# Sixteen conditioning products on another engine, and block-wise order around three norms, in a two-layer encoder trunk

## Chip, cores and metric

One core of a Trainium2 chip (the program uses 1 core). Time is device microseconds from first to last instruction as the runs give it, the median of several runs; lower is better. All numbers are fp32 (matmul operands are split into a high and a low part of type fp32r).

## What is computed

A trunk of two layers over 256 tokens of width 1024. Both layers are modulated by a conditioning vector:

```python
cond = jax.nn.silu(c)
mod = cond @ ada_w[l] + ada_b[l]                       # (1024) @ (1024, 6*1024)
sh_a, sc_a, g_a, sh_f, sc_f, g_f = jnp.split(mod, 6, axis=-1)
h = modulate(rms_norm(x, norm_attn[l]), sh_a, sc_a)    # h*(1+scale) + shift
y = diff_attention(h, ...)   if l == 0 else window_attention(h, ..., k_band, v_band)
x = x + g_a * y
h = modulate(rms_norm(x, norm_ffn[l]), sh_f, sc_f)
y = swiglu(h, ffn_w_in, ffn_w_out) if l == 0 else moe_swiglu(h, ...)   # 8 experts, top 2
x = x + g_f * y
# after layer 0: shared keys and values from modulate(rms_norm(x, kv_norm), ...) @ kv_w
```

The products of the title are `cond @ ada_w` for two of these rows: `sh_f` of layer 0 and `g_f` of layer 1. Each is a sum over eight pieces of 128x1024: piece k is scaled by a column of `condT` and added into a 128x1024 row block, which TensorE then sums over partitions with a matrix of ones (`mod_sums`).

## The kernel before

Five engines run programs of their own, ordered by semaphores alone; within an engine the written order holds. Tokens lie in two blocks of 128 (i = 0, 1).

**Weights.** SP loads everything of size into a ring of 12 slots of 128x1024 (`WRAW`), in the order that `ring_order()` writes out; a slot is reloaded when its reader is done (`slot_read`). ScalarE copies a unit to fp32r (`hi`, L675, into 6 slots of `WHI`), VectorE subtracts (`lo`, L1052, `WLO`), and TensorE runs three matmuls per product (`split_mm`, all at L1667: high x high, high x low, low x high). Units are numbered through: 0 to 23 query/key/value, 24 to 31 W_O of layer 0 (`U_WO`), 32 on the feed-forward (`U_FF`), then `U_KV`, `U_BQ` (queries of layer 1), `U_BO`, `U_MOE`. `hi` of a unit waits until TensorE has used the unit six before it.

**Conditioning pieces** share the ring: the places `(c, k)` are piece k of chunk c, `("gate_f", k)` those of layer 1's gate. VectorE multiplies and adds in one operation (L1066 `early_product`, L1076 `gate_products`, L1087 for the pieces that GpSimd loads into its own four slots); some pieces TensorE takes itself (`scale_pieces` in the first attention; in heads 9 to 12 it gives their slots free).

**Norms.** For each block: `residual` (L1214, L1215), the sum of squares and root on ScalarE (`norm_root`), `scaled` (L1114), `norm` (L1124), transposes on TensorE (`ht_transposes`, L1717), high parts on ScalarE (`ht_his`, L734) and low parts on VectorE (`ht_los`, L1135, or L1137 with a scale). `project_by_block` runs block 0's matmuls ahead of block 1's, so that block 0's residual and norm can begin early.

**Attention.** Heads n = 0 to 15 (8 heads, two row blocks) in a pipeline: TensorE logits for n + 3, VectorE bias and maximum for n + 2 (`biased`, L1168, L1172), ScalarE exponentials for n + 2 (L754), VectorE totals of n (L1182; in layer 0 also L1186 and L1188, which combine the two softmax maps), TensorE transposes (L1790), ScalarE copies (`copy_pt`, L764), TensorE products with V. `keep_clock` issues matmuls whose result nobody reads.

**Feed-forward.** 11 steps of 256 columns: in-projection (4 units), SiLU on ScalarE (L879), product on VectorE (L1348), transposes (L1936), high part (L883) and low part (L1352), out-projection (2 units). VectorE works off 64 further conditioning products in these steps; when one chunk is complete (`FF_SUMS`), TensorE sums it in two halves (`mod_half`) that ScalarE copies back (L889).

GpSimd issues some loads and clears rows with memsets (L569 to L622); it computes nothing else before the experts.

## Time and profile before

| | us |
|---|---|
| median of 3 runs | 1558.24 (1553.27 to 1561.35) |
| profiled execution | 1554.59, span of its instructions 1552.8 |
| TensorE busy | 1480.1 (95%), mean granted clock 0.979 of 2.4 GHz |
| VectorE, ScalarE, GpSimd busy | 1301.7 (84%), 980.2 (63%), 89.0 (6%) |
| DMA | 318 GB/s over the span |

Busy times are shares of the whole span and don't say which engine a stage waits for. That is read from the chain of work that ended last, from the table of stretches and from the waits within one stretch. A busy TensorE may still run at its lower clock: the mean granted clock of the stretch tells.

### The profile page before, as it was taken

How to read it: one execution, taken by the hardware profiler on the slowest of the kernel's cores; microseconds unless marked ns; L12 is line 12 of the kernel's file. 1: busy time of each engine (PE TensorE's matmuls, PEld its weight loads, DVE VectorE, ACT ScalarE, POOL GpSimd, SP SyncE). 2: the span in 40 equal slices, each digit the busy share in tenths (PEclk: the TensorE clock that was granted, in tenths of full speed). 3: DMA queues.
4: the chain of work that ended last, by engine and by line, in shares of the span. 5: the costliest groups of instructions: out<-in, count | busy, mean ns of one | idle time of the engine just before them, and what ended most of it. 6: DMA issues, size and time to landing. Idle time of an engine off the chain costs nothing.

```text
span 1552.8 us, 22121 instructions
## 1 busy us (share of the span) xinstructions
PE 1480.1 (95%) x6514; PEld 1159.6 (75%) x6514; DVE 1301.7 (84%) x1390; ACT 980.2 (63%) x1248; POOL 89.0 (6%) x127
## 2 busy tenths in 40 slices
PE   5997899999889889999999999999999999999998
PEld 2774677777567668888888888888888888888886
DVE  6787878887865687998888888889889888889897
ACT  2468343443544346777777776777677767777774
POOL 3000121120100001000000000000000000000100
PEclk9999999999995989999999999999999999999999
DMA  9983699998740279999999999999999999999993
GB/s 352 334 337 101 194 338 365 352 360 294 172 140 14 82 270 327 365 363 395 361 358 390 371 356 388 370 365 372 374 372 367 377 364 369 368 366 363 397 393 137
DMA packets 212225, 494.33 MB, mean 318 GB/s; under 512 B 16433, under 2 KB 39185, under 8 KB 212177
## 3 DMA queue, kind: packets, MB, share of 16 engines
q1 hardware_dynamic: 196848, 440.46, 78.3%
q0 software_dynamic: 14528, 51.22, 9.4%
q10 hardware_dynamic: 802, 2.06, 0.4%
q8 instruction: 25, 0.41, 0.1%
q14 instruction: 22, 0.18, 0.0%
HBM read 487.13 MB, written 6.55 MB: 318 GB/s over the span
## 4 chain that ended last, share of the span: by engine, by line
PE 84%; DVE 8%; DMA 3%; ACT 2%; issue 1%; SPq 0%; ACTq 0%; DVEq 0%
PE PS L1667 80%; DVE WLO L1052 2%; DMA WRAW<-in_a_w_qkv 2%; PE PS L2151 2%; DMA WRAW<-in_ada_w 1%; DVE MOD L1066 1%; PE PS L1790 1%; ACT WHI L675 1%; DVE HT_LO L1135 1%; DVE MOD L1076 1%; PE PS L1717 0%; PE PS L2129 0%; DVE ss L1142 0%; SPq L432 0%; DVE X L1215 0%
## 5 line engine op out<-in xcount | busy, mean ns | idle before, releaser
L1052 DVE TENSOR_TENSOR WLO<-WRAW,WHI 128x1024 fp32r<-128x1024 f32 x790 | 916.1, 1218 | 60.0 <-ACT WHI L675 59.7
L675 ACT ACTIVATE WHI<-WRAW 128x1024 fp32r<-128x1024 f32 x790 | 779.0, 1052 | 92.7 <-PE PS L1667 65.6
L1667 PE MATMUL PS<-WHI,HT_HI 128*128 128x512 f32 x1280 | 518.4, 405 | 25.7 <-DVE WLO L1052 17.8
L1667 PE MATMUL PS<-WLO,HT_HI 128*128 128x512 f32 x1280 | 509.2, 398 | 0.0
L1667 PE MATMUL PS<-WHI,HT_LO 128*128 128x512 f32 x1280 | 435.9, 397 | 0.0
L1667 PEld LDWEIGHTS PS<-WHI,HT_HI 128*128 128x128 f32 x1280 | 242.0, 189 | 88.0 <-DVE WLO L1052 21.2
L1667 PEld LDWEIGHTS PS<-WHI,HT_LO 128*128 128x128 f32 x1280 | 241.9, 189 | 59.0
L1667 PEld LDWEIGHTS PS<-WLO,HT_HI 128*128 128x128 f32 x1280 | 242.6, 190 | 54.7 <-issue 0.5
L1667 PE MATMUL PS<-WHI,AT_HI 128*128 128x512 f32 x536 | 216.7, 404 | 2.8 <-DVE AT_LO L1582 1.4
L1667 PE MATMUL PS<-WLO,AT_HI 128*128 128x512 f32 x536 | 211.7, 395 | 0.0
L1667 PE MATMUL PS<-WHI,AT_LO 128*128 128x512 f32 x536 | 211.7, 395 | 0.0
L994 ACT ACTIVATE AT_HI<-PS 128x512 fp32r<-128x512 f32 x56 | 33.5, 599 | 197.4 <-PE PS L2151 197.4
L1667 PEld LDWEIGHTS PS<-WHI,AT_HI 128*128 128x128 f32 x536 | 100.6, 188 | 30.0 <-issue 2.9
L1667 PEld LDWEIGHTS PS<-WLO,AT_HI 128*128 128x128 f32 x536 | 100.6, 188 | 26.8 <-issue 2.9
L1667 PEld LDWEIGHTS PS<-WHI,AT_LO 128*128 128x128 f32 x536 | 100.5, 188 | 24.5
L1582 DVE TENSOR_TENSOR AT_LO<-PS,AT_HI 128x512 fp32r<-128x512 f32 x56 | 38.8, 692 | 92.8 <-ACT AT_HI L994 92.8
L1087 DVE SCALAR_TENSOR_TENSOR MOD<-SHR,condT,MOD 128x1024 f32<-128x1024 f32 x64 | 81.9, 1279 | 2.1 <-DVE MOD L1087 0.5
L643 POOL DMA_DIRECT2D y_rows<-MOD x7 | 4.0, 574 | 792.8 <-DVE MOD L1561 792.8
L1667 PE MATMUL PS<-MOD,CST 128*128 128x512 f32 x64 | 34.9, 657 | 12.1 <-DVE MOD L1066 6.8
L1066 DVE SCALAR_TENSOR_TENSOR MOD<-WRAW,condT,MOD 128x1024 f32<-128x1024 f32 x32 | 41.0, 1281 | 6.5 <-DMA WRAW<-in_ada_w 5.7
L883 ACT ACTIVATE AT_HI<-PS 128x512 fp32r<-128x512 f32 x11 | 6.6, 599 | 60.4 <-PE PS L1936 60.4
L990 ACT ACTIVATE MOD<-PS 128x512 f32<-128x512 f32 x56 | 33.5, 599 | 15.3 <-PE PS L1667 15.3
(215 smaller groups left out, 841.8 us busy)
## 6 DMA issues: line engine op xcount, KB each, us to landing
WRAW<-in_moe_w_in SPq DMA_DIRECT2D x448, 512.0 KB, 6.4
WRAW<-in_moe_w_out SPq DMA_DIRECT2D x224, 512.0 KB, 5.5
WRAW<-in_ada_w SPq DMA_DIRECT2D x48, 512.0 KB, 8.8
SHR<-in_ada_w POOLq DMA_DIRECT2D x48, 512.0 KB, 6.6
WRAW<-in_ffn_w_in SPq DMA_DIRECT2D x88, 256.0 KB, 5.9
WRAW<-in_a_w_qkv SPq DMA_DIRECT2D x24, 512.0 KB, 15.4
WRAW<-in_ffn_w_out SPq DMA_DIRECT2D x22, 512.0 KB, 6.9
SHR<-in_kv_ada_w POOLq DMA_DIRECT2D x16, 512.0 KB, 6.3
```

Of the source, the lines that this page charges most:

```text
L675: nc.scalar.activation(WHI[:, u.split(k), :], WRAW[:, u.raw(k), :], ACT.Copy).then_inc(w_hi, 1)
L990: nc.scalar.activation(ESIL, PS[:, 0, :], ACT.Silu).then_inc(e_silu, 1)
L994: nc.scalar.activation(AT_HI[:, :], PS[:, 2, :], ACT.Copy).then_inc(e_at_hi, 1)
L1052: V_.tensor_tensor(WLO[:, u.split(k), :], WRAW[:, u.raw(k), :], f32(WHI[:, u.split(k), :]), ALU.subtract).then_inc(w_lo, 1)
L1066: V_.scalar_tensor_tensor(row, piece, condT[:, k:k + 1], row, ALU.mult, ALU.add).then_inc(ada_used, 1)
L1076: V_.scalar_tensor_tensor(row, WRAW[:, place % RAW_SLOTS, :], condT[:, k:k + 1], row, ALU.mult, ALU.add).then_inc(ada_used, 1)
L1087: V_.scalar_tensor_tensor(row, ADA[:, k % ADA_SLOTS, :], condT[:, k:k + 1], row, ALU.mult, ALU.add).then_inc(ada_used, 1)
L1135: V_.tensor_tensor(dst, src, high, ALU.subtract).then_inc(ht_lo, 1)
L1582: V_.tensor_tensor(AT_LO[:, :], PS[:, 2, :], f32(AT_HI[:, :]), ALU.subtract).then_inc(e_at, 1)
L1667: return nc.tensor.matmul(out, a, b, start=start, stop=stop)
L1790: last = nc.tensor.transpose(PS[:, 4 + n % 2, at:at + P], s_buf(a, n)[:, m, kt * P:(kt + 1) * P], ident)
L2151: last = nc.tensor.transpose(PS[:, 2, c * P:(c + 1) * P], EACT[:, c * P:(c + 1) * P], ident)
```

## The change

1. The eight pieces of layer 0's feed-forward shift, `(3, k)`, move ahead of W_O's units 28 to 31 in the ring, and their products from VectorE to GpSimd, into the first attention: a multiplication in place, then an addition to the row, with a wait on GpSimd's own semaphore after each. The eight `gate_f` products also move to GpSimd, into the second attention.
2. TensorE sums the shift row after block (0, 5) of W_O (`shift_sum`), no longer after (1, 2).
3. The first feed-forward step's SiLU and product run by block, and step 1's first two units are multiplied for each block as it is ready (`f_in_first`).
4. ScalarE copies the second half of each summed chunk (`mod_half(c, 1)`) behind the first two high parts of the next step.
5. Around the three norms of layer 0's end, the keys and layer 1's queries, the low parts of weights and of block 0 are reordered, on ScalarE and VectorE.
6. In the second attention Q's block 1 is transposed in two halves through one bank; in both, the square-root table is loaded one head earlier.

The core of the diff:

```diff
-    order += list(range(U_WO + 4, U_FF)) + [(3, k) for k in range(KT)]
+    order += [(3, k) for k in range(KT)] + list(range(U_WO + 4, U_FF))
     order += list(range(U_FF, U_BO + 5)) + [("gate_f", k) for k in range(KT)]
...
+POOL_PIECES = [(3, k) for k in range(KT)] + [("gate_f", k) for k in range(KT)]
+DVE_PIECES = [what for what in RING if isinstance(what, tuple) and what not in PE_PIECES and what not in POOL_PIECES]
...
-                elif isinstance(what, tuple):
-                    sp.wait_ge(ada_used, DVE_FF + what[1] + 1)
+                elif what in POOL_PIECES:
+                    sp.wait_ge(pool_used, POOL_PIECES.index(what) + 1)
                 elif place >= 0:
                     sp.wait_ge(w_lo, (what if what is not None else U_MOE + place - len(RING)) + 1)
...
+                    for piece in range(KT):
+                        load_piece((3, piece), t["ada_w"][0], 3 * D)
                 load(u, k, t["a_w_o"][0, k * P:(k + 1) * P, :])
-            for k in range(KT):
-                load_piece((3, k), t["ada_w"][0], 3 * D)
...
+            def pool_products(first, row):
+                for k in range(KT):
+                    n = first + k
+                    place = PLACE[POOL_PIECES[n]]
+                    pool.wait_ge(w_landed[place % RAW_SLOTS], landed_at(place))
+                    piece = WRAW[:, place % RAW_SLOTS, :]
+                    nc.gpsimd.tensor_scalar(piece, piece, condT[:, k:k + 1], None, ALU.mult).then_inc(pool_scaled, 1)
+                    pool.wait_ge(pool_scaled, n + 1)
+                    nc.gpsimd.tensor_tensor(row, row, piece, ALU.add).then_inc(pool_used, 1)
+                    pool.wait_ge(pool_used, n + 1)
+            pool.wait_ge(modb_landed, 32)
+            pool_products(0, MOD[:, MOD0[3], :])
             pool.wait_ge(attn["A"]["pt_psum"], TB * HEADS)
...
+            pool.wait_ge(attn["B"]["biased"], 1)
+            pool_products(KT, MOD[:, MOD1[5], :])
             pool.wait_ge(attn["B"]["pt_psum"], TB * HEADS)
...
-                    if n == 1 and a == "B":
-                        transposed(10, lambda n: Q[:, 1, n * 512:n * 512 + 512], 3, (6, 7), qkt_psum)
+                    if n in (1, 2) and a == "B":
+                        transposed(9 + n, lambda _: Q[:, 1, (n - 1) * 512:n * 512], 3, (7,), qkt_psum)
...
+                    if n == 13:
                         load_table(ACT.Sqrt)
...
             hi(u, 30, 31)
+            mod_rows(MOD0[3], 2, 4)
             hi_ff_in(u, (32,), 0, True)
             norm_root(0, 1)
-            mod_rows(MOD0[3], 2, 4)
             hi_ff_in(u, (33, 34), 0, True)
             ht_his(2, BLOCKS[:2])
             hi_ff_in(u, (35,), 0, True)
             norm_root(1, 2)
+            load_table(ACT.Silu)
             ht_his(2, BLOCKS[2:])
-            load_table(ACT.Silu)
...
+                u, it, k0 = Units(first + step // 2 * RAW_SLOTS), step // 2, 6 * (step % 2)
+                if step:
+                    hi_ff_in(u, range(k0, k0 + 2), it)
+                if step - 1 in FF_SUMS:
+                    mod_half(FF_SUMS[step - 1], 1)
+                hi_ff_in(u, range(k0 + 2, k0 + 4), it)
+                f_at(step + 1)
+                hi(u, k0 + 4, k0 + 5)
+                f_silu(u, k0 + 3)
+                if step in FF_SUMS:
+                    mod_half(FF_SUMS[step], 0)
             first = U_FF + FF_IN
-            for it in range((FF_STEPS - 1) // 2):
-                f_pair(it)
+            hi_ff_in(Units(first), range(0, 2), 0)
+            for i, (sem_in, n, sem_out) in enumerate(((f_block, 1, silu_block), (w_used, U_FF + FF_IN, silu_ready))):
+                act.wait_ge(sem_in, n)
+                nc.scalar.activation(FSIL[:, i, :], PS[:, i, 0:FC], ACT.Silu).then_inc(sem_out, 1)
+            for step in range(FF_STEPS - 1):
+                f_step(step)
             u = Units(U_KV - FF_OUT)
             hi(u, 0, 1)
+            mod_half(FF_SUMS[FF_STEPS - 2], 1)
+            hi(u, 2, 3)
             f_at(FF_STEPS)
-            hi(u, *range(2, 6))
+            hi(u, 4, 5)
...
-            ht_his(4, BLOCKS[:2])
             act.wait_ge(kv_block, 1)
             nc.scalar.activation(KV[:, 0, :], PS[:, 4, :], ACT.Copy).then_inc(kv_copied, 1)
-            ht_his(4, BLOCKS[2:])
+            ht_his(4, BLOCKS[:2])
+            hi(u, 2)
             act.wait_ge(w_used, U_BQ)
             nc.scalar.activation(KV[:, 1, :], PS[:, 6, :], ACT.Copy).then_inc(kv_copied, 1)
-            hi(u, 2, 3)
+            ht_his(4, BLOCKS[2:])
+            hi(u, 3, 4)
             for i in range(TB):
                 act.wait_ge(kv_copied, i + 1)
                 block_squares(i, KV[:, i, 0:256], 7)
-            hi(u, 4, 5, 6)
+            hi(u, 5, 6, 7)
             transposed(0, lambda n: KBT[:, 2 * n:2 * n + 2, :].rearrange("p j k -> p (j k)"), 4,
                        range(0, 2), kbt_psum)
-            hi(u, 7)
...
-            lo_and_products(29, 1)
             o_scale(1)
-            for piece in islice(rest, 1):
-                early_product(piece)
+            lo(u, 29)
             ht_los(1, BLOCKS[2:], gcol[:, 2:3])
-            for piece in islice(rest, 2):
-                early_product(piece)
-            lo_and_products(30, 1)
-            lo_and_products(31, 3)
+            lo(u, 30, 31)
...
-            lo(u, 32)
+            lo(u, 32, 33)
             ht_los(2, BLOCKS[:2])
-            lo(u, 33)
+            lo(u, 34)
             dve.wait_ge(w_used, U_FF)
             residual(1, MOD0[2])
+            lo(u, 35)
             scaled(1, H, MOD0[4], 2, 2)
-            lo(u, 34)
             rms(1)
             norm(1, H, MOD[:, MOD0[3], :])
-            lo(u, 35)
+            lo(u, 36)
             ht_los(2, BLOCKS[2:])
+            lo(u, 37)
...
+            for i, (ready, done) in enumerate(((silu_block, act_block), (silu_ready, act_ready))):
+                dve.wait_ge(ready, 1)
+                V_.tensor_tensor(FACT[:, i, :], FSIL[:, i, :], PS[:, i, FC:2 * FC], ALU.mult).then_inc(done, 1)
...
+                    if step or k >= 2:
+                        lo(u, k0 + k)
...
             lo(u, 0, 1)
-            f_at(FF_STEPS)
             dve.wait_ge(mod_ready, MOD_READY_EARLY + 2 * LATE_SHIFT_F)
             fold(MODKV[1], MOD[:, MODKV[1], :], 3)
-            lo(u, 2)
+            lo(u, 2, 3)
+            f_at(FF_STEPS)
+            lo(u, 4, 5)
             dve.wait_ge(block_out, 2)
             residual(0, MOD0[5])
             scaled(0, H, MODKV[1], 3, 3)
             rms(0)
             norm(0, H, MOD[:, MODKV[0], :])
-            lo(u, 3)
-            ht_los(3, BLOCKS[:2])
             dve.wait_ge(w_used, U_KV)
             residual(1, MOD0[5])
+            ht_los(3, BLOCKS[:2])
             scaled(1, H, MODKV[1], 3, 4)
-            lo(u, 4)
             rms(1)
             norm(1, H, MOD[:, MODKV[0], :])
-            lo(u, 5)
+            fold(MOD1[1], MOD[:, MOD1[1], :], 4)
             ht_los(3, BLOCKS[2:])
-            fold(MOD1[1], MOD[:, MOD1[1], :], 4)
             u = Units(U_BQ)
-            for i in range(TB):
-                scaled(i, Q, MOD1[1], 4, 3 + i)
-                norm(i, Q, MOD[:, MOD1[0], :])
-                lo(u, i)
-            ht_los(4)
-            lo(u, 2, 3)
+            scaled(0, Q, MOD1[1], 4, 3)
+            norm(0, Q, MOD[:, MOD1[0], :])
+            lo(u, 0)
+            ht_los(4, BLOCKS[:2])
+            lo(u, 1)
+            scaled(1, Q, MOD1[1], 4, 4)
+            norm(1, Q, MOD[:, MOD1[0], :])
+            lo(u, 2)
+            ht_los(4, BLOCKS[2:])
+            lo(u, 3, 4)
...
-            lo(u, *range(4, 8))
+            lo(u, 5, 6, 7)
...
-            lo(u, 13)
-            gate_products(0, 1)
-            lo(u, 14)
-            gate_products(2, 3)
-            lo(u, 15)
+            lo(u, 13, 14, 15)
...
-            gate_products(4, 5)
-            lo(u, 18)
-            gate_products(6, 7)
-            lo(u, 19)
+            lo(u, 18, 19)
...
-                    if n == 1 and a == "B":
+                    if n in (1, 2) and a == "B":
                         pe.wait_ge(qk_norm, 6)
-                        block_transposes(Q, 1, 6, qkt_psum)
+                        if n == 2:
+                            pe.wait_ge(qkt_ready, 11)
+                        for h in range(4):
+                            c = (n - 1) * 512 + h * P
+                            last = nc.tensor.transpose(PS[:, 7, h * P:(h + 1) * P], Q[:, 1, c:c + P], ident)
+                        last.then_inc(qkt_psum, 1)
+                    if n == 3 and a == "B":
                         pe.wait_ge(qkt_ready, 12)
                     if n:
                         products(n - 1)
                     if a == "A":
                         scale_pieces(n)
-                    elif 2 <= n < HEADS:
+                    elif 3 <= n < HEADS:
                         keep_clock(7, 1)
...
+            def shift_sum():
+                pe.wait_ge(ht_lo, 8)
+                mod_sums(KT, MOD0[3], 2, pool_used)
             project_by_block(Units(U_WO), 4, 4, {
                 (0, 2): second_rows,
-                (1, 2): lambda: mod_sums(DVE_EARLY, MOD0[3], 2),
+                (0, 5): shift_sum,
                 (1, 6): lambda: ht_transposes(H, h_parts(2, BLOCKS[:2]))})
...
+            def f_in_first(u):
+                for i, ready in enumerate((act_block, act_ready)):
+                    pe.wait_ge(ready, 1)
+                    for k in range(2):
+                        split_ready(u, k)
+                        s, rows = u.split(k), slice(i * P, i * P + P)
+                        for kt in range(2):
+                            cols, kk = slice(kt * 512, kt * 512 + 512), 2 * k + kt
+                            last = split_mm(PS[:, i, :], HT_HI[:, kk, rows], HT_LO[:, kk, rows], WHI[:, s, cols],
+                                            WLO[:, s, cols], kk == 0, False)
+                        if i:
+                            last.then_inc(w_used, 1)
...
+                    if it or b:
+                        pe.wait_ge(act_ready, it * 2 + (b + 1))
+                        f_in(u, 6 * b, (0, 1))
+                    else:
+                        f_in_first(u)
...
+                if k == 1:
                     ht_transposes(Q, h_parts(4, BLOCKS[:2]))
             ht_transposes(Q, h_parts(4, BLOCKS[2:]))
...
+            mod_sums(len(POOL_PIECES), LATE_SLOTS[LATE_GATE_F], 2, pool_used)
```

## Rows read from the trace of the kernel before

**Rows 1.** The page, chain that ended last: shares of the span by engine.

```profile
PE 84%; DVE 8%; DMA 3%; ACT 2%; issue 1%; SPq 0%; ACTq 0%; DVEq 0%
```

**Rows 2.** Stretches: length, busy of PE, PEld, DVE, ACT, POOL (instructions); clock; DMA.

```profile
107.00:155.00 48.00, 38.69 (x200) 22.45 (x198) 37.59 (x91) 36.55 (x112) 0.57 (x1) 1.00 0.45 161
155.00:212.00 57.00, 48.47 (x201) 37.05 (x201) 45.84 (x48) 21.37 (x30) 12.35 (x14) 0.94 0.69 223
212.00:391.00 179.00, 178.08 (x761) 138.62 (x760) 151.66 (x139) 74.11 (x90) 30.09 (x57) 1.00 0.94 342
391.00:458.00 67.00, 54.28 (x235) 40.24 (x234) 48.59 (x60) 33.46 (x48) 6.84 (x8) 0.95 0.64 170
458.00:511.00 53.00, 48.52 (x238) 36.67 (x236) 27.31 (x69) 29.53 (x91) 0.57 (x1) 0.68 0.11 33
511.00:566.00 55.00, 46.54 (x212) 35.44 (x212) 44.40 (x72) 20.59 (x31) 1.09 (x2) 0.88 0.43 144
566.00:1552.80 986.80, 977.86 (x4338) 787.59 (x4338) 863.81 (x829) 717.34 (x787) 21.49 (x18) 1.00 0.98 360
```

**Rows 3.** Waits of PE in 155 to 212: total us, times, longest.

```profile
PE PS L1667 <- DVE WLO L1052: 6.8, 3, 3.2
PE PS L1667 <- DVE MOD L1066: 0.9, 1, 0.9
```

**Rows 4.** Waits of PE in 212 to 391.

```profile
PE PS L1667 <- DVE WLO L1052: 0.9, 5, 0.2
```

**Rows 5.** Waits of PE in 391 to 458.

```profile
PE PS L1667 <- DVE WLO L1052: 8.0, 3, 3.1
PE PS L1667 <- ACT MOD L931: 1.2, 1, 1.2
```

**Rows 6.** Waits of PE in 458 to 511, then in 511 to 566.

```profile
PE PS L1667 <- ACT Q L742: 1.9, 1, 1.9
PE PS L1667 <- DVE WLO L1052: 2.0, 1, 2.0
```

**Rows 7.** DVE by line, 155 to 185: busy us, mean ns, idle.

```profile
L1066 DVE SCALAR_TENSOR_TENSOR MOD<-WRAW,condT,MOD 128x1024 f32<-128x1024 f32 x8 | 10.2, 1280 | 0.3
```

**Rows 8.** Timeline of DVE and PE: start us, us, engine, line, operation.

```profile
175.36 1.22 DVE L1214 TENSOR_TENSOR H<-PS,MOD 128x1024 f32<-128x1024 f32 x1
...
553.31 0.29 PE L2088 MATMUL PS<-CST,W 8*128 8x8 f32 x2
...
555.16 0.17 DVE L1461 TENSOR_TENSOR rt<-PS,rb 128x16 f32<-128x16 f32 x1
```

**Rows 9.** Groups of DVE by line, 511 to 566.

```profile
L1052 DVE TENSOR_TENSOR WLO<-WRAW,WHI 128x1024 fp32r<-128x1024 f32 x9 | 10.9, 1217 | 0.1
L1076 DVE SCALAR_TENSOR_TENSOR MOD<-WRAW,condT,MOD 128x1024 f32<-128x1024 f32 x8 | 10.2, 1281 | 0.4
L1124 DVE SCALAR_TENSOR_TENSOR H<-H,nx,MOD 128x512 f32<-128x512 f32 x4 | 2.8, 749 | 0.1
```

**Rows 10.** SP and ACT in first attention; landing times of loads, 130 to 152.

```profile
137.22 2.68 SPq L432 DMA_DIRECT2D WRAW<-in_ada_w  x2
WRAW<-in_ada_w SPq DMA_DIRECT2D x4, 512.0 KB, 3.7
139.07 1.05 ACT L675 ACTIVATE WHI<-WRAW 128x1024 fp32r<-128x1024 f32 x1
148.20 1.28 ACT L696 ACT_TABLE_LOAD   x1
```

**Rows 11.** Timeline of POOL: its memsets.

```profile
160.73 4.46 POOL L600 MEMSET MOD<- 128x2048 f32 x3 [11.68 <-DVE Q L1151]
191.91 2.67 POOL L602 MEMSET MOD<- 128x3072 f32 x1 [26.71 <-DVE H L1124]
```

**Rows 12.** Groups of DVE by line in first attention, 107 to 155.

```profile
L1168 DVE TENSOR_TENSOR S<-PS,SHR 128x256 f32<-128x256 f32 (+1 forms) x8 | 4.4, 556 | 2.6 <-PE PS L1667 2.3
L1188 DVE SCALAR_TENSOR_TENSOR S<-S,sm 128x128 f32<-128x128 f32 (+1 forms) x8 | 3.3, 418 | 0.3
```

69 lines of the change are left out of this document (24 added, 45 removed).

## The prediction

> **What bounds the kernel now.** I read the chain that ended last first: TensorE carries 84% of it, VectorE 8% [rows 1]. So a microsecond counts only where TensorE stands still or runs at its lower clock. The table of stretches shows where that is [rows 2]: the experts (566 to 1552.8) are full (977.9 of 986.8 us busy, clock 1.00), and the change doesn't touch them. The feed-forward steps are full too (178.1 of 179.0). What is loose lies in five stretches: first attention (107 to 155, 9.3 us of TensorE idle), its output projection and the first feed-forward block (155 to 212: 8.5 idle, mean clock 0.94), key/value and query projection (391 to 458: 12.7 idle, clock 0.95), second attention (458 to 511: 4.5 idle, clock 0.68) and its output projection with the router (511 to 566: 8.5 idle, clock 0.88). A mean clock of 0.94 over 57 us is 3.4 us of full-speed time lost, 0.95 over 67 us also 3.4; the two levels are 2.4 and 1.2 GHz. The pitch of matmuls at full clock comes from the full stretch: 178.08 us over 761, 0.234 us each [rows 2]. Then I asked TensorE's waits in each stretch who ended them [rows 3 to 6]: nearly all are low parts (`lo`, L1052) that VectorE makes late.
>
> **Feed-forward's shift products to GpSimd, and the output projection (155 to 212).** Removed from VectorE: eight products, 10.2 us, mean 1280 ns [rows 7]. That isn't 10.2 us of path: TensorE stood 0.9 us for the last of them and 6.8 for low parts [rows 3], the shortest of them behind a product, the two long ones (up to 3.2) from the order around the norm and the first SiLU. `residual(0)` began at 175.36 [rows 8], after the products and the fold, though its matmuls were done some 2 us earlier. With the products gone and low parts 32 and 33 done ahead, and with the first SiLU split so that step 1's first matmuls (`f_in_first`) fill the time of SiLU and product, the waits of 6.8 and 0.9 and the 3.4 us of lost clock are up for gain: 11.1. What is late next: `f_in_block(0, 2)` is followed by the transposes of block 1's norm. From the end of W_O, VectorE needs two residual operations, a low part, a scaling and a norm: 4 x 1.22 + 2 x 0.75 = 6.4 us [rows 9]; TensorE has three blocks of 6 matmuls, 18 x 0.234 = 4.2. So a wait of 2.2 remains, and up to 3.8 with `lo(34)` and `ht_los` ahead of the residual; I take 3.0, and as such a wait was followed by the low clock before, half of the lost clock, 1.7. **Term: 11.1 - 4.7 = -6.4** (bounds -11 and -3).
>
> **What moves in the queues for it.** On SP the eight shift pieces pass ahead of W_O units 28 to 31. These then hold ring places that are free only when TensorE has used the four scale pieces in heads 9 to 12; before, four of the shift pieces waited there, the first issued at 137.22 and landing 3.7 us later [rows 10]. So unit 28 lands at 140.9, while ScalarE took it at 139.07 [rows 10]: ScalarE's strict order puts 1.9 us of waiting in front of the next heads' exponentials and PT copies. It runs two heads ahead, so the bounds are 0 and +1.9; I take +1.5. The feed-forward loads behind them on SP no longer wait for VectorE's low parts and products, but stand behind GpSimd's. Loading the square-root table one head earlier takes 1.28 us [rows 10] from between the last head's transposes and products: -1.2 (bounds -1.3 and 0). On GpSimd's queue the products pass ahead of the wait for the gain `norm_ffn`; they cost nothing as long as they end before attention does.
>
> **How long GpSimd takes, and what that does to VectorE.** No row shows GpSimd reading. The nearest are its memsets: 2.67 us for 3072 columns, 0.89 for 1024 [rows 11]. A product is now a multiplication (one in, one out) and an addition (two in, one out): with all streams overlapped 2 x 0.89 = 1.8 us, with each stream paid singly 5 x 0.89 = 4.5. I take the middle, 3.1, so 25 us for eight (14 to 36). The Trainium skill (GPSIMD Engine Reference, § 3.1) gives 4497 ns for an addition of 2048 columns, by estimate 2.25 us here, and § 4.1 there advises VectorE for such work; the sum would be the same by it, and no run here shows it yet. First set: the pieces land about when attention begins, 107, and their sum stands behind eight blocks of 6 matmuls of W_O, 155 + 8 x 1.4 = 166: 59 us, 7.4 per product. Second: 458 to 553, 12 per product. Both hide.
>
> But attention's VectorE work runs beside it. VectorE's products kept 1280 ns beside GpSimd's memsets (4.46 us at 160.73) and 1281 in a stretch where GpSimd did next to nothing [rows 7, 9, 11]: writing alone disturbs nothing, and a pure reading of the rows gives 0. Reading isn't shown. In first attention each head has an L1186 and an L1188 (0.42 us), which read two operands from SBUF [rows 12]. If these wait once per head for half of a mean GpSimd operation (0.8 us) over the ten heads that 25 us cover, that is 8 us, less about half of the idle time VectorE has there (2.6 us in the eight heads of one buffer [rows 12], so some 4 in ten): +4. Bounds 0 and +14 (below). **Term of first attention: 1.5 - 1.2 + 4 = +4.3.**
>
> **Sums of the feed-forward steps.** `mod_half(c, 1)` on ScalarE goes behind the first two `hi` of the next step. TensorE's waits for low parts in these steps are 0.9 us in all [rows 4]. **-0.9** (0 to -2).
>
> **Key/value and query projection.** The three long waits for low parts (8.0 us) and one for the copy of KV (1.2) [rows 5] go: `lo(4)` comes before the head norms, `hi(7)` before the copies of the transposed keys, and ScalarE copies KV ahead of block 1's high parts. With shorter gaps the 3.4 us of clock return. New waits: `ht_los(3)` of block 0 now stands behind both operations of `residual(1)`, 2.4 us, and ahead of it one low part less, 1.2: +1.2. Between the norms of Q's two blocks VectorE has two low parts, two `ht_los`, a scaling and a norm of two halves: 3 x 1.22 + 4 x 0.75 = 6.7 us (each half operation at the norm's 0.75 [rows 9]), while TensorE has 12 matmuls, 2.8, and 8 shorter transposes, some 4 us: +2.7. One of the low-clock stretches I leave: +1.2. **Term: -12.6 + 5.1 = -7.5** (-12.6 to -4).
>
> **Second attention.** The half-by-half transposes of Q's block 1 remove the 1.9 us wait for the copies [rows 6]. Heads run on TensorE at a clock of 0.68 on average [rows 2], so nothing else there ends a wait, and GpSimd's products meet no VectorE operation with two SBUF inputs but `lo(12)`. **-1.9** (-4 to 0).
>
> **Gate products to GpSimd (511 to 566).** Again 10.2 us leave VectorE [rows 9], and of the path: the 2.0 us for `lo(15)` behind four of them [rows 6], and the start of the router's logits, which came at 555.16 behind the last four, while the transposes that feed them were issued at 553.31 and took 0.29 [rows 8]: 1.4. The wait for the norm of block 1 stays. **-3.4** (-3.4 to -2). The expert weights that wait for these ring places land earlier; no wait there was for a load, so 0.
>
> **Sum:** 4.3 - 6.4 - 0.9 - 7.5 - 1.9 - 3.4 = **-15.8 us**. On the profiled execution of 1554.59 (span 1552.8) that is 1538.8; on the median of the runs, 1558.24 (3.65 above it, among runs from 1553.27 to 1561.35), 1542.4. I forecast **1540**, between the two.
>
> **Rivals.** *A: GpSimd's reading and VectorE's two-operand operations shut each other out for whole instructions.* Then each head's L1186 waits for the rest of one GpSimd operation (0.8 us) and L1188 for a whole one (1.55), as the two stand close enough for GpSimd to step in between: 2.35 a head, over some seven heads until the 25 us are worked off, 16, less 2 of idle: +14 instead of +4, **1550**. For it: the operations are there in every head; against it: rows 7 and 9, which only show writing. The Trainium skill (SBUF — State Buffer, § Who interferes with whom) states this exclusion for a VectorE instruction with two SBUF inputs against a GpSimd instruction that reads SBUF, and none against one that only writes; with the second half the trace agrees (1280 against 1281 ns). *B, the slower side: a GpSimd product takes over 10 us.* Then the first set ends after 166 and TensorE waits in the middle of W_O: 8 x (T - 7.4). At T = 10.7 this is 26 us, which turns the sum into +10: some **1566**; from T = 9.4 on the change is a loss. That would be 12 memset passes per product, against it the 0.89 of rows 11. *C: the change doesn't do what it says in the two norm stretches*: TensorE stops at the next norm instead of at low parts, and the clock falls there as before. Half of 6.4 and 7.5 is then lost, +7: **1547**. For it: the mean clocks of 0.94 and 0.95 stand beside waits of 3 us, and one of my new waits is that long. *D: no exclusion (-4) and no lost clock or wait left behind the new norms (-5):* **1531**.
>
> **Chances.** Forecast 0.49, A 0.20, B 0.06, C 0.18, D 0.07. The range 1527 to 1552 leaves out B, the worse third of A and a little below D: about 0.16. What can be told from no change is about 0.5%, 7.8 us: under 1550.4 is faster. Of A a bit under half is faster, of C most: faster 0.49 + 0.07 + 0.09 + 0.15 = 0.80, same 0.14, slower 0.06.
>
> **What would show it.** GpSimd rows of 128x1024 beside first attention, each pair near 3.1 us, ending before 155; L1186 or L1188 with idle time ahead of them ended by nothing on the chain (A). `hi` of unit 28 some 2 us late behind its load. In the W_O stretch no wait for L1066, one of about 3 us for L1124 (C if longer, with the clock down). In 391 to 458 no wait over 1 us for L1052. Router logits right behind their transposes. Wrong would be: experts at another pace, a longer second attention, or the sum of the shift rows as the releaser of a TensorE wait (B).

## The result, and the profile after

The changed kernel takes 1543.86 us in the median (1529.26 to 1553.59), the kernel before 1559.71 in the same series. Ratio **0.9888, 95% interval 0.9866 to 0.991**: faster by some 17 us. The ratio leaves out the two slowest runs of the changed kernel (1553.55 and 1553.59), which count as slow; with them the medians differ by 15.9 us. The forecast was 1540 with 1527 to 1552. What I had not foreseen is the spread: 24 us for the changed kernel, where the kernel before has 12 (1553.27 to 1565.04, one outlier apart). The first profiled execution of the changed kernel (1553.59) was its slowest, so the rows below, wherever they are called "after", are from another execution of the same kernel, `e1_again`, with a span of 1538.5.

The stretches of the kernel after, cut where the same stages now begin; columns as in [rows 2]:

```profile
107.00:160.00 53.00, 39.33 (x196) 22.33 (x194) 45.06 (x89) 35.07 (x111) 44.53 (x17) 0.97 0.47 170
160.00:217.00 57.00, 51.66 (x224) 40.73 (x225) 40.14 (x46) 24.52 (x35) 12.88 (x15) 0.97 0.65 215
217.00:395.00 178.00, 176.42 (x757) 138.21 (x756) 157.78 (x144) 77.49 (x94) 32.85 (x61) 1.00 0.97 350
395.00:447.00 52.00, 47.18 (x215) 35.77 (x213) 40.08 (x53) 27.54 (x41) 3.74 (x4) 0.97 0.62 167
447.00:499.00 52.00, 49.23 (x236) 38.11 (x235) 27.27 (x68) 29.52 (x91) 42.21 (x17) 0.64 0.35 121
499.00:554.00 55.00, 47.94 (x227) 37.09 (x228) 36.45 (x66) 22.50 (x33) 1.08 (x2) 0.91 0.33 106
```

Against [rows 2], first attention is longer (53 us to the first matmul of the output projection, 48 before), GpSimd is busy for 44.5 us of it, and the projection of keys, values and queries is much shorter. Second attention has the lowest clock, 0.64. TensorE's waits after, in four groups: output projection with the first feed-forward block (160 to 217), feed-forward, key/value and query projection, and the stage behind second attention (499.3 to 576.8):

```profile
PE PS L1726 <- DVE H L1140: 2.7, 1, 2.7
PE PS L1676 <- DVE HT_LO L1151: 2.2, 1, 2.2
PE PS L1676 <- DVE HT_LO L1153: 1.2, 1, 1.2
...
PE PS L1676 <- DVE AT_LO L1364: 1.6, 1, 1.6
...
PE PS L1676 <- DVE HT_LO L1151: 2.4, 1, 2.4
PE PS L1726 <- DVE Q L1140: 1.8, 1, 1.8
PE PS L1726 <- DVE H L1140: 0.6, 1, 0.6
...
PE PS L1726 <- DVE H L1140: 3.2, 1, 3.2
PE PS L1676 <- DVE HT_LO L1151: 2.2, 2, 1.2
PE PS L1676 <- DVE HT_LO L1576: 2.2, 1, 2.2
...
```

Not one wait for weights' low parts (L1052 before, L1078 now) is left of the 6.8, 0.9, 8.0 and 2.0 us of [rows 3 to 6], nor one for the shift products. What stands there now are waits for norms (L1140) and for the low parts of transposes.

Where the time went is clearest in the length of each stage, from the first matmul of one to the first matmul of the next in TensorE's timeline. The borders are: first matmul of the output projection; first and last matmul of the feed-forward's output blocks; clock matmuls ahead of second attention; first matmul of its output projection; first expert output. "Rest" runs to the end of the span. The kernels are described below.

| profiled execution | to output proj. | + first FF block | FF | KV, Q | attention B | to experts | rest | span |
|---|---|---|---|---|---|---|---|---|
| before | 155.1 | 62.6 | 180.2 | 61.0 | 52.7 | 81.1 | 960.2 | 1552.8 |
| after, first | 168.6 | 55.9 | 178.9 | 54.4 | 55.7 | 77.0 | 961.4 | 1551.8 |
| after (e1_again) | 160.4 | 56.7 | 178.5 | 51.8 | 51.9 | 77.6 | 961.6 | 1538.5 |
| e2_shift_dve | 154.5 | 59.8 | 178.7 | 51.6 | 54.0 | 77.5 | 961.4 | 1537.5 |
| e3_gate_dve | 165.0 | 55.9 | 178.8 | 51.6 | 54.0 | 81.2 | 961.3 | 1547.7 |
| e7_kv_undone | 161.5 | 56.7 | 178.2 | 61.1 | **37.0** | 77.2 | 960.0 | 1531.6 |
| e8_fill | 165.2 | 55.9 | 179.1 | 54.4 | **37.0** | 76.0 | 961.5 | 1529.0 |
| e9_best | 156.2 | 60.6 | 178.5 | 51.8 | **37.0** | 76.3 | 961.5 | 1521.9 |
| e10_before_fill | 158.5 | 62.7 | 180.2 | 61.1 | 52.7 | 81.1 | 961.6 | 1557.8 |

### The profile page after: what moved, and what is told of

Read it like the earlier page. It is cut to its first block, busy times and chain, and to the rows that moved or that the text cites. A ratio compares the mean times of both kernels' runs of the same rounds, so it can differ in the third digit from the quotient of the medians.

```text
span 1551.8 us, 22142 instructions
## 1 busy us (share of the span) xinstructions
PE 1488.7 (96%) x6513; PEld 1170.5 (75%) x6513; DVE 1291.8 (83%) x1375; ACT 980.5 (63%) x1249; POOL 175.0 (11%) x159
## 4 chain that ended last, share of the span: by engine, by line
PE 89%; DVE 6%; DMA 2%; ACT 1%; issue 1%; SPq 0%; POOL 0%; DVEq 0%; ACTq 0%
PE PS L1676 85%; PE PS L2190 2%; DMA WRAW<-in_ada_w 1%; PE PS L1799 1%; DVE WLO L1078 1%; PE PS L1726 1%; DMA SHR<-in_kv_ada_w 1%; DVE MOD L1092 1%; DVE MOD L1103 0%; DVE sm L1202 0%; DVE HT_LO L1151 0%; PE PS L2168 0%; DVE X L1231 0%; DVE ss L1158 0%; DVE H L1230 0%
## 5 line engine op out<-in xcount | busy, mean ns | idle before, releaser
L1078 DVE TENSOR_TENSOR WLO<-WRAW,WHI 128x1024 fp32r<-128x1024 f32 x790 | 915.6, 1217 | 43.4 <-ACT WHI L696 42.9
L606 POOL TENSOR_SCALAR WRAW<-WRAW,condT 128x1024 f32<-128x1024 f32 x16 | 47.5, 2967 | 74.3 <-DMA WRAW<-in_ada_w 37.2
```

Of the source, the lines that this page charges most:

```text
L606: nc.gpsimd.tensor_scalar(piece, piece, condT[:, k:k + 1], None, ALU.mult).then_inc(pool_scaled, 1)
L1078: V_.tensor_tensor(WLO[:, u.split(k), :], WRAW[:, u.raw(k), :], f32(WHI[:, u.split(k), :]), ALU.subtract).then_inc(w_lo, 1)
```

## The experiments

Three questions were open: what lengthens first attention, whether each stage's gain belongs to the part that I gave it to, and where the spread comes from. The theories that the text names by a letter are set out in the expectations.

**1. The same kernel again, and one part undone at a time.**

> The changed kernel once more, for another profiled execution. In the profile at hand first attention ends 13.5 us later than before (output projection begins at 168.6 instead of 155.1), at a mean granted clock of 0.89. Theory R (GpSimd's reading holds up VectorE's operations with two SBUF operands, the heads come slower and the clock falls at chance places): the time again between 1529 and 1553 us, ratio 0.985 to 0.993, and a faster execution has the same VectorE gaps in first attention but a higher clock there. Rival Q (what is lost is the late load of output-projection unit 28 and the order on SP): the gap in front of hi(28) on ScalarE is the largest one there, 2 us or more, whatever the clock.

Ratio 0.9918 (0.9889 to 0.9948), median of ten runs 1546.30 us (1536.14 to 1551.59). The wait for unit 28 is there, 1.11 us ahead of `hi(28)` on ScalarE, but it isn't the largest gap. TensorE's waits in first attention, after (107 to 160) and, in the last two lines, before (107 to 155):

```profile
PE PS L1799 <- DVE MOD L1204: 6.4, 5, 2.2
PE PS L1799 <- DVE S L1204: 3.8, 3, 1.6
PE PS L1799 <- ACT H L801: 1.6, 1, 1.6
...
PE PS L1790 <- DVE MOD L1188: 3.0, 3, 1.1
PE PS L1790 <- DVE S L1188: 1.8, 2, 1.2
...
```

10.2 us in eight places for VectorE's combination of a head, where the kernel before waits 4.8 in five for the same step (L1188). This execution has such gaps as the first profiled one has (10.7 us in seven places there), and a mean clock of 0.97, where the first has 0.83 over its longer attention (107 to 168; the 0.89 of the expectation is the mean up to 155). That speaks for theory R.

`e2_shift_dve` gives the shift products back to VectorE (the core of the edit; the order on SP and the place of the row's sum go back too):

```diff
-POOL_PIECES = [(3, k) for k in range(KT)] + [("gate_f", k) for k in range(KT)]
+POOL_PIECES = [("gate_f", k) for k in range(KT)]
...
+            lo_and_products(29, 1)
             o_scale(1)
-            lo(u, 29)
...
-            lo(u, 30, 31)
...
+            lo_and_products(30, 1)
+            lo_and_products(31, 3)
```

> The changed kernel with the eight shift products (3, k) back on VectorE behind attention, with their pieces behind output-projection units 28 to 31 on SP and their row sum in block 1's pass, as before the change; gate products stay on GpSimd, everything else stays changed. Theory R: first attention is as before (output projection begins at about 154 to 156 us), and the stage after it loses the 6.7 us that it gained; together about 7 us faster than the changed kernel: ratio to the kernel before about 0.984. If the attention's loss of some 10 us is not due to the GpSimd products at all (the earlier square-root table, say): output projection begins at 165 or later and the time is 6 us above the changed kernel's, ratio 0.993.

Ratio 0.9842 (0.9766 to 0.9918), 1535.71 us. First attention is as before (154.5 against 155.1), the next stage takes 59.8 instead of 56.7. So of the 5.9 us that this stage gained, the products' leaving is worth 3.1; the other 2.8 come from the order and the halved first SiLU, which this kernel keeps (a remainder; they were not undone singly). Against that, first attention loses 6.0 by these two executions, one low-clock stretch of some 3 us (124 to 127) in `e1_again` included. **On balance the shift products on GpSimd cost 2.9 us**, more where the clock falls. I had expected 7. The ratio is the expected one, 0.984, but four runs between 1522.35 and 1543.68 don't settle it; the stages do.

`e3_gate_dve` gives the gate products back:

```diff
-            lo(u, 13, 14, 15)
+            lo(u, 13)
+            gate_products(0, 1)
+            lo(u, 14)
+            gate_products(2, 3)
+            lo(u, 15)
```

> The changed kernel with the eight gate products back on VectorE in the output projection behind second attention, as before the change; shift products stay on GpSimd. My forecast's term for these was -3.4 us (2.0 for lo(15), 1.4 for the router's logits) and nothing lost in second attention: so 3.4 us slower than the changed kernel, ratio to the kernel before about 0.991. Rival: GpSimd's reading costs second attention about 3 us as well (it ended at 512.3 against 510.4 with a wait of 1.9 gone): then equal to the changed kernel within 1 us, and second attention ends at about 509.

The stage behind second attention takes 81.2 us again, 81.1 before and 77.6 with the products on GpSimd: the 3.6 us belong to them. TensorE's wait of 2.0 for the low part is back. Second attention takes 54.0 without GpSimd's work and 51.9 and 55.7 with it, and VectorE's scaling of a head's output there (L1210, one operand in PSUM) takes 292 ns with GpSimd's products beside it and 291 without: nothing shows that GpSimd costs time there. The total doesn't tell it: ratio 0.9918 (0.9888 to 0.9947), equal to the changed kernel's, which is what the rival said. But the interval is 9 us wide, the effect 3.6, for a reason that comes in part 3. TensorE's waits behind second attention in this run:

```profile
PE PS L1693 <- DVE WLO L1078: 2.0, 1, 2.0
...
PE PS L1693 <- DVE rt L1499: 1.1, 1, 1.1
```

**2. What lengthens first attention.** `e4_write_only` puts six writes in place of a multiplication and an addition in the first eight products; the shift row is left out (in the three diffs of this part the semaphores, and in the first two the condition that keeps the gate products as they are, are left out):

```diff
-                    nc.gpsimd.tensor_scalar(piece, piece, condT[:, k:k + 1], None, ALU.mult).then_inc(pool_scaled, 1)
-                    nc.gpsimd.tensor_tensor(row, row, piece, ALU.add).then_inc(pool_used, 1)
+                    for m in range(6):
+                            pool.memset(piece, 0.0)
```

> In the changed kernel each of the first eight GpSimd products (a multiplication and an addition, 5.4 us) is replaced by six writes of a constant into the same piece, some 0.89 us each, 5.4 us; the products of the shift row of block 0's feed-forward are left out. SP's order, the ring places and when they come free stay the same. Theory R (reading is what hurts): first attention is back to its length before, output projection begins at 154 to 157 us, some 10 to 13 us faster than the changed kernel, ratio to the kernel before 0.979 to 0.983. Rival Q (late load of unit 28, order on SP), or a GpSimd that disturbs by writing too: it still begins at 165 or later, and the ratio is that of the changed kernel, 0.989.

VectorE's groups between 117 and 160 us, first of the kernel after (L1202 is the scalar step of each head's totals, one column of two operands; L1204 the combination), then of this one, then GpSimd's own groups after and here (105 to 170):

```profile
L1202 DVE SCALAR_TENSOR_TENSOR sm<-sm,neglam 128x1 f32<-128x1 f32 x15 | 10.7, 711 | 0.5
L1204 DVE SCALAR_TENSOR_TENSOR S<-S,sm 128x256 f32<-128x256 f32 (+1 forms) x7 | 3.1, 437 | 0.2
...
L1209 DVE SCALAR_TENSOR_TENSOR sm<-sm,neglam 128x1 f32<-128x1 f32 x15 | 3.3, 219 | 0.5
...
L606 POOL TENSOR_SCALAR WRAW<-WRAW,condT 128x1024 f32<-128x1024 f32 x8 | 25.1, 3138 | 37.4 <-DMA WRAW<-in_ada_w 36.7
L608 POOL TENSOR_TENSOR MOD<-MOD,WRAW 128x1024 f32<-128x1024 f32 x8 | 18.8, 2350 | 0.7
...
L610 POOL MEMSET WRAW<- 128x1024 f32 x48 | 45.7, 952 | 40.1 <-DMA WRAW<-in_ada_w 37.4
```

GpSimd is as busy (45.7 us against 43.9), and the one-column step falls from 711 ns back to 219. The last transposes of first attention end at 148.6, as in `e2_shift_dve` (148.3), 154.3 with the products. So it is the reading, and the late load of unit 28, which is in this kernel too (1.31 us of waiting on ScalarE), costs some 0.3 us, an estimate from these two ends. The output projection began at 158.6, not at 154 to 157: the granted clock was 0.50 from 150 to 156. Ratio 0.9885 (0.983 to 0.9941), 1537.56 us, not the 0.979 to 0.983 expected. The verdict rests on the rows, not on the time. It holds over all fourteen profiles of this document: the last transposes end at 148.2 to 150.4 in the six in which GpSimd reads nothing beside first attention, and at 154.3 to 159.9 in the eight in which it does.

Which instruction of GpSimd does it? VectorE at one head, then GpSimd beside it, after:

```profile
120.67 0.42 DVE L1188 TENSOR_REDUCE sm<-S 128x2 f32<-128x256 f32 x1
121.01 0.15 DVE L1198 RECIPROCAL sm<-sm 128x2 f32<-128x2 f32 x1
121.20 1.57 DVE L1202 SCALAR_TENSOR_TENSOR sm<-sm,neglam 128x1 f32<-128x1 f32 x1
122.80 0.37 DVE L1204 SCALAR_TENSOR_TENSOR MOD<-MOD,sm 128x128 f32<-128x128 f32 x1
...
117.37 2.95 POOL L606 TENSOR_SCALAR WRAW<-WRAW,condT 128x1024 f32<-128x1024 f32 x1
120.40 2.35 POOL L608 TENSOR_TENSOR MOD<-MOD,WRAW 128x1024 f32<-128x1024 f32 x1
122.85 2.95 POOL L606 TENSOR_SCALAR WRAW<-WRAW,condT 128x1024 f32<-128x1024 f32 x1
```

One-operand instructions (L1188, L1198) run on beside the addition, with the lengths that they have before (0.42 and 0.15 us). L1202 ends at 122.77, when the addition ends at 122.75. The blocked time is inside the instruction's own duration, not idle time ahead of it, which was the sign that I had named for rival A. All seven L1202 that met an addition took 1.07 to 1.57 us, all nine that met a multiplication 0.22. So I expected that two inputs on both sides are needed, and tested it with multiplications alone (`e5_one_input`; the shift row is left out):

```diff
-                    nc.gpsimd.tensor_tensor(row, row, piece, ALU.add).then_inc(pool_used, 1)
+                    nc.gpsimd.tensor_scalar(piece, piece, condT[:, k:k + 1], None, ALU.mult).then_inc(pool_used, 1)
```

> In the changed kernel, GpSimd's addition (two inputs from SBUF) of the first eight products is replaced by a second multiplication of the piece in place (one input from SBUF); the shift row of block 0's feed-forward is so left out. GpSimd is busy as long or longer: 2 x 2.85 against 2.85 + 2.35 us a product. Theory R1, from the trace of the changed kernel (L1202 took 0.22 us in each of the nine heads in which it met GpSimd's multiplication, and 1.07 to 1.57 in the seven in which it met the addition, until the addition's end): only instructions with two inputs on both engines shut each other out. Then L1202 keeps 0.22 us in all heads, the last transposes of first attention end at about 148.5 us as with writes alone (148.57) instead of 154 to 160, and the ratio to the kernel before is about 0.983. Rival R2 (any GpSimd instruction that reads): L1202 is 0.7 us on average or more, the last transposes end at 154 or later, ratio 0.99.

R1 fell in this form. The step takes 452 ns in the mean, between both theories, and the combinations (L1210 here) are longer too:

```profile
L1208 DVE SCALAR_TENSOR_TENSOR sm<-sm,neglam 128x1 f32<-128x1 f32 x15 | 6.8, 452 | 0.5
L1210 DVE SCALAR_TENSOR_TENSOR S<-S,sm 128x256 f32<-128x256 f32 (+1 forms) x7 | 4.4, 633 | 0.2
...
133.50 2.86 POOL L609 TENSOR_SCALAR WRAW<-WRAW,condT 128x1024 f32<-128x1024 f32 x1
133.75 1.15 DVE L1210 SCALAR_TENSOR_TENSOR S<-S,sm 128x256 f32<-128x256 f32 x1
...
136.45 2.85 POOL L607 TENSOR_SCALAR WRAW<-WRAW,condT 128x1024 f32<-128x1024 f32 x1
136.58 1.25 DVE L1210 SCALAR_TENSOR_TENSOR S<-S,sm 128x256 f32<-128x256 f32 x1
```

Take the instruction's own 0.48 off its end: 133.75 + 1.15 - 0.48 = 134.42, or 0.92 after the multiplication's start; 136.58 + 1.25 - 0.48 = 137.35, 0.90 after it. So it is in all nine cases of this run (0.90 to 0.95); those that came over 0.9 us after a multiplication's start were not held up. The multiplication shuts VectorE out for its first 0.9 of 2.85 us, the addition for 2.15 of 2.35 (the same working on the 13 cases of the two profiles of the changed kernel: 2.14 to 2.16). These shares go by GpSimd's spans in the profile, which its legend calls rough; from start to start the two take 3.03 and 2.45 in the rows above. In the profile of the changed kernel that I had read, VectorE's two-operand steps came 0.05 us ahead of a multiplication or 1.2 us and more after its start, never in between; so it looked harmless. (In the first profile two combinations came within 0.1 us of a multiplication's start; they took 1.16 and 1.23 instead of 0.35, which gives 0.90 and 0.91.) Ratio 0.9872 (0.9817 to 0.9928). The last transposes end at 154.6, not at R1's 148.5, with the clock at half from 135 to 139 and again from 152.

If the lock lasts as long as an instruction, shorter additions should help. `e6_add_parts`:

```diff
+                    for c in range(4):
+                        cols = slice(c * D // 4, (c + 1) * D // 4)
-                        nc.gpsimd.tensor_tensor(row, row, piece, ALU.add)
+                        nc.gpsimd.tensor_tensor(row[:, cols], row[:, cols], piece[:, cols], ALU.add)
```

> In the changed kernel each of GpSimd's sixteen additions is cut into four of 256 columns, one behind the other; what is computed stays. If a VectorE instruction with two SBUF inputs only waits for the GpSimd instruction that is running, L1202 waits 0.6 us at most (a quarter of 2.35) instead of up to 2.35, its mean falls from 0.71 to about 0.4, first attention's last transposes end at about 150 instead of 154, and the kernel is about 4 us faster than the changed kernel: ratio to the kernel before 0.984 to 0.987. Rival: the next part begins before VectorE comes in, so L1202 still waits for the last part, at a cost per part of its own (some 0.1 us each): ends at 154 or later, ratio 0.99 or above.

The step's mean fell to 409 ns as expected, but the combinations behind it took 686 and 911 instead of 424 and 437: VectorE gets in between two parts and is shut out again by the next. All three groups together cost 18.0 us against 17.2 with whole additions (9.6 undisturbed), and an addition takes 4 x 0.76 = 3.0 us. The last transposes end at 159.3, with the clock down three times before that (from 120, 127 and 140). Ratio 0.9876 (0.9818 to 0.9933), 1540.91 us: no gain that can be told.

**3. The key/value projection, and the spread.** `e7_kv_undone` puts back the order before on three engines, for example on VectorE:

```diff
-            scaled(0, Q, MOD1[1], 4, 3)
-            norm(0, Q, MOD[:, MOD1[0], :])
-            lo(u, 0)
-            ht_los(4, BLOCKS[:2])
-            lo(u, 1)
+            for i in range(TB):
+                scaled(i, Q, MOD1[1], 4, 3 + i)
+                norm(i, Q, MOD[:, MOD1[0], :])
+                lo(u, i)
+            ht_los(4)
```

> The changed kernel with VectorE's, ScalarE's and TensorE's order in the key/value and query projection as before the change (from the last feed-forward step's high parts to the copies of the transposed keys); all else stays changed. My term for this stage was -7.5 us; by the two profiles it is some 9 (from the last feed-forward output matmul to the clock matmuls of second attention: 61.0 us before, 51.8 after). If that is the order's own worth: the stage takes 60 to 62 us again and the kernel is 9 us slower than the changed kernel, ratio to the kernel before 0.995 to 0.998. If most of it were the granted clock's chance: 56 us or less, ratio 0.992 or below.

The stage takes 61.1 us again, with the waits of [rows 5] (8.1 for low parts, 1.2 for the copy). So the 9.2 us are the order's own. (It is 6.6 in the executions in which this stage took 54.4 us, with a second low-clock stretch in it: the first profile and `e8_fill`.) The ratio, 0.9933 (0.9902 to 0.9964), is 2 us worse than that of `e1_again` and 7 worse than that of the first series, in an interval of 10: the total doesn't settle it. And the profiled execution is the shortest so far, 1531.6: in it second attention took 37.0 us instead of 52 to 56. The two stretches of second attention, after and here (length, TensorE busy, clock, DMA share, GB/s):

```profile
447.43:499.31 51.88, 48.80 (x233) 0.64 0.35 119
...
457.47:494.43 36.96, 32.76 (x234) 1.00 0.35 115
```

The same heads, with GpSimd's products beside them in both (41.8 and 35.8 us busy); the granted clock is 0.64 in one and 1.00 in the other. At 0.50 TensorE is busy almost without a break (25.00 of 25.00 us in a row further down) and bounds the heads. Where the clock falls, it does so soon after the first head's start; after:

```profile
453.02 0.44 PE L1799 MATMUL PS<-CST,MOD 128*128 128x128 f32 x2 [1.66 <-ACT MOD L775]
453.39 0.49 PE L1676 MATMUL PS<-MOD,Q 64*128 64x128 f32 x4
453.81 0.44 PE L1799 MATMUL PS<-CST,MOD 128*128 128x128 f32 x2
454.08 0.60 PE L1834 MATMUL PS<-CST,Q 128*128 128x128 f32 x4
454.83 1.12 PE L1676 MATMUL PS<-MOD,W 128*128 128x64 f32 x4
```

The last row takes 1.12 us, where the same four matmuls take 0.66 at full clock: 1.8 us after a wait of 1.66 the clock is at half. So I filled that wait, in the changed kernel:

```diff
+                    if n == 0 and a == "B":
+                        keep_clock(5, 7)
                     transposes(n)
```

> The changed kernel with seven more clock matmuls on TensorE (1.64 us at full clock) between the first logits of second attention and head 0's transposes, where every profile has a wait of 1.66 us for ScalarE. In six of the seven profiles of changed kernels the granted clock fell to 0.50 within some 3 to 10 us of that wait and stayed there for most of the stage, which took 52 to 56 us; in one (order of the key/value projection undone) it stayed at 1.00 and the stage took 37.0. Theory S (the wait opens the way for the fall; whether it comes is chance): with the wait filled the clock stays at 1.00, the stage takes 37 to 39 us, the kernel some 14 us less than most executions of the changed kernel: 1527 to 1533, ratio to the kernel before 0.978 to 0.983, with less spread. Rival (the heads themselves are too thin for the higher clock): the clock falls all the same, the stage takes 52 or more, ratio 0.989.

**1530.19 us, 1528.87 to 1531.36**, ratio 0.9833 (0.9794 to 0.9872). The stage takes 36.95 us at a clock of 1.00:

```profile
454.52:491.47 36.95, 34.42 (x241) 1.00 0.38 125
```

The four runs lie within 2.5 us. (Of the profiles named in the expectation it is seven of eight that fell, not six of seven.) Theory S holds for this stage: 37 us or some 52 to 56. By the ratios the filling is worth 8.6 to 13.3 us (0.9833 against 0.9888 and 0.9918). How much of the changed kernel's spread is this stage is shown only in part. By their mean granted clocks, 0.988 and 0.985, where the four runs here have 0.987 to 0.989, probably only the two fastest of its twenty runs kept the clock in it. The other eighteen, 0.967 to 0.981, still lie between 1535.52 and 1553.59. The profiles show three more variable parts: first attention with its gaps (output projection from 160.4 to 168.9), the key/value stage (51.6 to 54.4) and this stage with the clock down (51.9 to 55.7).

> As the run before, and one clock matmul a head also in the last eight heads of second attention, where TensorE waited up to 0.7 us a head at full clock; before, only heads 3 to 7 had one. Theory S: no further gain, as the clock is at 1.00 already; ratio the same within 0.003. Rival (the heads are too thin): this one holds the clock where the run before does not, 12 us or more faster than that. If the clock falls in spite of it, the eight matmuls cost 0.3 to 0.4 us each at half clock on the path, 3 us more than the run before.

(`elif 3 <= n < HEADS` becomes `elif n >= 3`.) 1529.37 us, ratio 0.9827 (0.9789 to 0.9866): the same, as theory S says; this stage took 38.3. One of its four runs, the profiled one, took 1535.52: there first attention lasted until 168.9.

Would the kernel before have gained as much? `e10_before_fill` is the kernel before with those two lines:

> The kernel before with only the seven clock matmuls ahead of head 0's transposes in second attention. There a second wait of 1.90 us follows one head later (for ScalarE's copies of Q's transposes), which the change removes. Theory S1 (any such wait opens the way for the fall): the clock still falls there, the stage takes 51 to 53 us, time as before, ratio 0.997 to 1.002; the removed wait was then a condition for holding the clock. Rival S2 (only the first wait matters): the stage takes 38 to 40 us and the kernel some 13 us less than before, ratio 0.990 to 0.993; then filling would have been worth nearly the same without the change, and the change is worth some 13 us at a held clock (1530.2 with the same filling).

Ratio 0.9992 (0.9979 to 1.0006), no difference. The clock is at 1.00 across the filled place and falls behind the second wait, the one of [rows 6]:

```profile
466.28 1.88 PE L1667 MATMUL PS<-AT_HI 128*128 128x512 f32 x7
468.01 0.44 PE L1790 MATMUL PS<-CST,MOD 128*128 128x128 f32 x2
...
472.00 0.66 PE L1667 MATMUL PS<-MOD,W 128*128 128x64 f32 x4 [1.89 <-ACT Q L742]
...
475.00:500.00 25.00, 25.00 (x101) 0.50 0.08 22
```

That is S1. The half-by-half transposes, which I had given 1.9 us, remove this wait, and with one wait left instead of two there is a chance that second attention runs at full clock: 15 us. (The kernel before isn't wholly without that chance, it seems: two of its 72 runs, 1546.97 and 1548.18, stand 12 and 8 us below the medians of their series, at mean clocks of 0.985 and 0.983. No profile shows in which stage.)

**4. A faster version.** 

> The seven clock matmuls together with the shift products back on VectorE (the rest of the change kept): 3 us less in first attention and output projection than with the shift products on GpSimd by the profiles (first feed-forward output matmul at 214.3 against 217.1), so by theory S 1522 to 1530 us, ratio to the kernel before 0.975 to 0.980; by the rival 0.984 to 0.987.

**1523.14 us (1521.30 to 1523.79), ratio 0.9785 (0.9747 to 0.9824)**, 7 us below `e8_fill`: with the shift products on VectorE first attention ends 9.0 us earlier in these two executions, and the stage behind it takes 4.7 longer; key/value took 2.6 less.

> The kernel with shift products back on VectorE and second attention filled (1523.1 us), with seven clock matmuls also ahead of head 0's transposes in first attention, where a wait of 1.61 us for ScalarE stands in every profile; in five of the eleven profiles of changed kernels the clock fell within 10 us of it. Theory S: no fall between 110 and 130 us, the last transposes of first attention end at 148.3 instead of 150.1, 1.5 to 2 us less than without, 1520 to 1522, ratio to the kernel before 0.976 to 0.979. Rival (the fall there comes from the heads' thin work): a fall as often as before, and no difference.

1524.12 us, ratio 0.9779 (0.9763 to 0.9795): no difference, and no verdict on the theory. The seven matmuls came to stand behind the wait, which sits ahead of the loop of heads; the 1.61 us remained, head 0's transposes came 1.7 us later, and the last transposes ended at 150.4, not at 148.3. The clock didn't fall in this execution.

## Why the prediction was right

The sum, -15.8, is close to the median's -15.9 and the ratio's -17.5. Part of that is luck. In the execution of 1538.5 the stages add up to -14.3, each within 2 us of its term; in the first profiled one they add up to -1.0, with +13.5 in first attention and +3.0 in second. The median lies in a spread of 24 us that no term of the sum has. By stage, with the terms beside the lengths of the table (after, span 1538.5):

- **First attention: +4.3 forecast, +5.4 measured, 5.4 to 13.8 in the six profiles that leave this stage as changed.** Mis-sized, and its parts more than the sum. The product takes 5.5 us from start to start (2.95 and 2.35 with what lies between), not 3.1, so GpSimd works some 44 us beside all sixteen heads, not 25 beside ten. Exclusion costs up to 6.0, not 4. The late load makes ScalarE wait 1.1 to 1.3 us but costs some 0.3, not 1.5. The earlier table gives 0.75 (last transposes to output projection 6.87 before, 6.12 in `e2_shift_dve`), not 1.2. Up to 8 us more come from the falling clock, which the term left out. Some of that is not the change's: in the kernel before, the output projection begins at 155.1 in one profile and at 158.5 in the other, `e10_before_fill`, whose first attention is the same and whose clock falls twice in it.
- **Rival A was right on the mechanism and wrong on its rule.** Two-operand instructions of VectorE are shut out by GpSimd's reading, as the Trainium skill (SBUF — State Buffer, § Who interferes with whom) says, and not by its writing (219 ns in `e4_write_only`); the trace agrees. But not for whole instructions: 0.9 of 2.85 us of a multiplication, 2.15 of 2.35 of an addition. The measurement decides. And L1204 rarely pays, since L1202 in front of it has already waited.
- **Output projection and first feed-forward block: -6.4, measured -5.9.** The waits of 6.8 and 0.9 went. The norm's wait is 2.7 (3.0 forecast), the clock 0.97 of 57 us, 1.7 lost, as forecast. A wait of 2.2 us for low parts of transposes (L1151) was not in the term. The forecast put most of it down to the products; they are worth 3.1.
- **Feed-forward: -0.9, measured -1.7.** Where the other 0.8 comes from stays open.
- **Key/value and query: -7.5, measured -9.2, and -6.6 where the clock falls twice.** All named waits went. The new ones are 2.4 and 1.8 with 1.6 of clock, near the 1.2, 2.7 and 1.2 of the forecast; but the residual's wait was not all new: 1.2 for L1135 stood there before (last line below), so I charged it twice.
- **Second attention: -1.9, measured -0.8 to +3.0, or -15.7 when the clock holds.** The step that failed: from a mean clock of 0.68 I concluded that "nothing else there ends a wait". The low clock was itself what bounded the heads, and the wait that goes was one of two that it followed. The other, 1.66 us for ScalarE, stands in the trace of the kernel before (first line below) and not in [rows 6]; I had overlooked it. My range, 25 us wide, didn't come from this: it held the median although it knew neither the stage's two lengths nor the clock's part in first attention.
- **Gate products: -3.4, measured -3.6.** Here the named parts were right too: `e3_gate_dve` brings back the 2.0 us and a wait for the router's logits of 1.1. Not in the term: the wait for the low parts of the first expert's tokens behind them (L1567 before, L1576 now) grows from 0.6 to 2.2, and the mean clock rises from 0.88 to 0.91.
- **Experts and end: 0 forecast.** The rest is 960.0 to 961.6 us in kernels with the change and without it (960.2 and 961.6), with the same pitch of expert steps.

The two waits of the kernel before at the start of second attention, then the one in its key/value stage:

```profile
464.36 0.44 PE L1790 MATMUL PS<-CST,MOD 128*128 128x128 f32 x2 [1.66 <-ACT MOD L754]
...
468.36 0.66 PE L1667 MATMUL PS<-MOD,W 128*128 128x64 f32 x4 [1.90 <-ACT Q L742]
...
PE PS L1667 <- DVE HT_LO L1135: 1.2, 1, 1.2
```

Rival B is out (5.5 against 9.4 us). C is half true: the waits for norms are there and the clock falls, but less than before in the two norm stretches. D's time was reached by `e8_fill`, in another way.

## What to carry to other kernels

A mean clock far under 1.00 in a stage need not be a property of its work: here the same heads ran at 1.00 once the waits ahead of the fall were filled or removed, all of them. Look for these before anything else in such a stage is costed. Work given to GpSimd was free here beside VectorE's one-operand and PSUM instructions, and where GpSimd only wrote. Otherwise price each VectorE instruction with two operands in SBUF at the rest of GpSimd's addition or of the first 0.9 us of its multiplication, and look for that time inside the instruction's duration. Where totals of one kernel spread by 20 us, the lengths of stages decide what a part is worth, not the totals.

## What the runs showed of the hardware

- GpSimd's multiplication of 128x1024 in place takes 2.84 to 3.08 us (the first of a run 3.9 to 4.2) and shuts out two-operand VectorE instructions in its first 0.90; its addition with two inputs takes 2.35 and shuts them out for 2.15, all by the profile's spans. The one with fewer inputs is the slower. Memsets of 0.95 us each left VectorE's one-column step at 219 ns.
- VectorE's instructions with one operand, or with one of two in PSUM, took 0.42 us (256 columns) and 0.69 us (512) beside GpSimd's products as in the kernel before.
- Four additions of 256 columns take 3.0 us where one of 1024 takes 2.35, and VectorE gets one instruction in between two of them.
- The same stage of 16 heads ran 36.95 us at a granted clock of 1.00 (2.4 GHz) and 52 to 56 with most of it at 0.50 (1.2 GHz). The fall followed a wait of TensorE of 1.66 us, or one of 1.89 where the first was filled; in one of eight profiles of changed kernels with the wait open the clock held. What else decides whether it falls stays open.
